# Down projection of a feed-forward layer: seven 2x2-block products in place of eight, for the first four k-tiles of seven column pairs

## The chip, the cores and the metric

The kernel runs on one core of a Trainium2 chip. The metric is the device time of one execution in microseconds (us). TensorE (PE) multiplies matrices into eight PSUM banks of 128 x 512 fp32, VectorE (DVE) and ScalarE (ACT) do elementwise work, GpSimd (POOL) and SyncE (SP) here mostly start transfers, and 16 DMA engines carry these out.

## The reference

Two blocks run one after the other on 256 tokens of width 2048, in fp32. The part that matters is the feed-forward layer at the end of the second block:

```python
        hn = rmsnorm(x, norm_ffn_pre[l])
        u = jnp.square(jax.nn.relu(jnp.einsum('bsd,df->bsf', hn, w_up[l])))
        y = jnp.einsum('bsf,fd->bsd', u, w_down[l])
        x = x + rmsnorm(y, norm_ffn_post[l])
```

Here w_up is 2048 x 8192 and w_down 8192 x 2048. Everything ahead of it (the gated MLP, two attention branches, an mLSTM and their projections) is untouched.

## The kernel before

**Precision.** An fp32 weight is used as two fp32r parts. ACT writes the high part (`wh`, line 561), DVE subtracts it from the weight and writes the low part (`wl`, line 1052). Tokens are kept as high and low parts too (`yth`, `ytl` for the inputs of the down projection). A product takes three matmuls: token high x weight low (line 1931), high x high (1932), token low x weight high (1933).

**Groups.** Weights come in groups of two k-tiles (256 rows) by 512 columns, 512 KB each, by one transfer of SP into one of five `stage` buffers (line 374). With two k-tiles, two halves of the tokens (128 each) and three matmuls, a group is 12 matmuls of 128 x 128 by 512 columns. Group j uses split buffer j modulo 5: ACT's part of group j waits until PE has finished group j-5 (semaphore `used`), DVE's part waits for ACT (`hi`), PE for DVE (`lo`), and the load of group j+5 waits for DVE's part of group j. 914 groups run in a fixed order, a chunk of 512 columns after the other, eight groups to a chunk of 16 k-tiles.

**The feed-forward layer** runs in four blocks q of 2048 hidden columns: chunks ("up", q, 0 to 3), then ("down", q, 0 to 3), which sum over this block's 16 k-tiles. Chunks alternate between PSUM banks 0, 1 and 2, 3, one bank for each half of the tokens. After an up chunk, ACT applies relu and square (lines 1002, 1005), DVE transposes it in 32 x 32 blocks (line 1092), SP sends it with four transfers of 128 KB into `ytl` (line 388), ACT makes the high part `yth` (line 589) and DVE the low one (line 1080). After a down chunk DVE copies or adds the two banks into `dacc` (lines 1801 and 1803); in block 3 it also multiplies by a row of gains (line 1806) that POOL has loaded into `rowb` (line 518).

**Order.** Each engine's program is written out by hand and runs strictly in order. `slot(n)` puts the splits of all groups up to n+3 ahead of the step that follows it, and `end(...)` is the group after a chunk's last. A step that waits holds up all that stands behind it on its engine.

## Time and profile before

| what | value |
|---|---|
| device time, median of 3 runs (lowest to highest) | 2576.77 us (2576.63 to 2576.93) |
| the profiled execution: its time, its span | 2578.93 us, 2577.2 us |
| busy: PE, weight loads of PE, DVE, ACT, POOL | 2571.3, 2131.7, 1582.6, 1246.6, 34.8 us |
| granted TensorE clock | full in all 40 slices |

The span runs from the first to the last instruction that the profiler saw; 1.73 us of the profiled execution lie around it. Busy time of PE is the time in which some matmul is under way, and matmuls overlap, so that the spacing of their starts, not their duration, tells how long one takes. Times in the rows are counted from the start of the span.

### The profile page before, as it was taken

The page shows a single profiled execution, that of the slowest core. Times are in us where ns is not written, and L with a number is a line of the kernel's source. Part 1 is how long each engine was busy: PE and PEld are TensorE (multiplying, and loading weights), DVE is VectorE, ACT ScalarE, POOL GpSimd, SP SyncE. Part 2 cuts the span into 40 slices and gives each one's busy share as a digit, 9 for nine tenths or more (in the row PEclk, how much of TensorE's full clock was granted, in tenths as well). Part 3 has the DMA queues.
Part 4 walks back from the last instruction along what each step waited for, and adds up shares of the span by engine and source line. Part 5 has one row for each costly group of instructions (what it writes and reads, how often), then busy time and mean ns, then how long its engine had stood idle before and what let it go on. Part 6 is the DMA issues. An engine that isn't in the chain of part 4 may idle for free.

```text
span 2577.2 us, 29181 instructions
## 1 busy us (share of the span) xinstructions
PE 2571.3 (100%) x11503; PEld 2131.7 (83%) x11503; DVE 1582.6 (61%) x1842; ACT 1246.6 (48%) x1495; POOL 34.8 (1%) x56
## 2 busy tenths in 40 slices
PE   9999999999999999999999999999999999999999
PEld 7888888888888888888888888888888888888887
DVE  5646565566666566676866876556575555555555
ACT  6554443444555555455544444444464354454453
POOL 1000000000000000000000000000010000000000
PEclk9999999999999999999999999999999999999999
DMA  8767766676777777777565877666566676676674
GB/s 273 205 193 208 205 205 192 199 205 199 216 217 198 211 207 199 223 224 218 168 187 167 222 215 216 203 200 197 192 212 215 194 202 218 186 217 208 196 223 151
DMA packets 534793, 527.41 MB, mean 205 GB/s; under 512 B 294896, under 2 KB 297824, under 8 KB 534656
## 3 DMA queue, kind: packets, MB, share of 16 engines
q1 hardware_dynamic: 531856, 518.09, 67.5%
q0 software_dynamic: 2384, 6.93, 1.1%
q8 instruction: 91, 1.49, 0.2%
q10 hardware_dynamic: 416, 0.52, 0.1%
q14 instruction: 46, 0.38, 0.0%
HBM read 488.24 MB, written 2.10 MB: 190 GB/s over the span
## 4 chain that ended last, share of the span: by engine, by line
PE 99%; DMA 0%; DVE 0%; ACT 0%; issue 0%; SPq 0%
PE bank L1931 32%; PE bank L1933 32%; PE bank L1932 32%; PE bank L2080 1%; PE bank L2069 1%; PE bank L2059 1%; PE bank L2002 0%; DMA t_stage<-in_a_w_in_dram 0%; PE bank L2015 0%; PE bank L2008 0%; PE bank L2140 0%; PE bank L2127 0%; PE bank L1993 0%; PE bank L2160 0%; PE bank L2153 0%; PE bank L2208 0%
## 5 line engine op out<-in xcount | busy, mean ns | idle before, releaser
L1052 DVE TENSOR_TENSOR t_wl<-t_stage,t_wh 128x1024 fp32r<-128x1024 f32 x912 | 1105.5, 1221 | 818.7 <-ACT t_wh L561 816.7
L561 ACT ACTIVATE t_wh<-t_stage 128x1024 fp32r<-128x1024 f32 x913 | 957.2, 1057 | 969.3 <-PE bank L1933 962.4
L1931 PE MATMUL bank<-t_wl,t_xth 128*128 128x512 f32 x2480 | 972.1, 392 | 0.4 <-DVE t_xtl L1073 0.4
L1933 PE MATMUL bank<-t_wh,t_xtl 128*128 128x512 f32 x2480 | 965.2, 389 | 0.0
L1932 PE MATMUL bank<-t_wh,t_xth 128*128 128x512 f32 x2480 | 965.0, 389 | 0.0
L1931 PEld LDWEIGHTS bank<-t_wl,t_xth 128*128 128x128 f32 x2480 | 465.7, 188 | 96.7 <-DVE t_xtl L1073 0.9
L1933 PEld LDWEIGHTS bank<-t_wh,t_xtl 128*128 128x128 f32 x2480 | 465.5, 188 | 96.9
L1932 PEld LDWEIGHTS bank<-t_wh,t_xth 128*128 128x128 f32 x2480 | 465.7, 188 | 96.0 <-issue 0.2
L1931 PE MATMUL bank<-t_wl,t_yth 128*128 128x512 f32 x1026 | 399.2, 389 | 0.0
L1932 PE MATMUL bank<-t_wh,t_yth 128*128 128x512 f32 x1026 | 398.7, 389 | 0.0
L1933 PE MATMUL bank<-t_wh,t_ytl 128*128 128x512 f32 x1026 | 398.7, 389 | 0.0
L1932 PEld LDWEIGHTS bank<-t_wh,t_yth 128*128 128x128 f32 x1026 | 192.6, 188 | 39.9
L1933 PEld LDWEIGHTS bank<-t_wh,t_ytl 128*128 128x128 f32 x1026 | 192.6, 188 | 39.9
L1931 PEld LDWEIGHTS bank<-t_wl,t_yth 128*128 128x128 f32 x1026 | 192.6, 188 | 39.7
L1092 DVE STREAM_TRANSPOSE t_pool<-t_pool 128x512 f32<-128x512 f32 x96 | 99.3, 1073 | 0.0
L1080 DVE SCALAR_TENSOR_TENSOR t_ytl<-t_ytl,t_yth 128x1024 fp32r<-128x1024 f32 x32 | 39.2, 1224 | 57.3 <-ACT t_yth L589 57.1
L589 ACT ACTIVATE t_yth<-t_ytl 128x1024 fp32r<-128x1024 f32 x32 | 33.9, 1061 | 64.2 <-DMA t_ytl<-t_pool 63.8
L1931 PE MATMUL bank<-t_wl,t_mth 128*128 128x512 f32 x128 | 49.9, 390 | 0.0
L1933 PE MATMUL bank<-t_wh,t_mtl 128*128 128x512 f32 x128 | 49.8, 389 | 0.0
L1932 PE MATMUL bank<-t_wh,t_mth 128*128 128x512 f32 x128 | 49.8, 389 | 0.0
L706 ACT ACTIVATE t_pool<-bank,t_scl 128x512 f32<-128x512 f32 x32 | 20.3, 686 | 26.0 <-PE bank L1933 25.9
L1002 ACT ACTIVATE t_pool<-bank,t_scl 128x512 f32<-128x512 f32 x32 | 20.3, 685 | 22.5 <-PE bank L1933 22.4
(304 smaller groups left out, 946.0 us busy)
## 6 DMA issues: line engine op xcount, KB each, us to landing
t_stage<-in_a_w_in_dram SPq DMA_DIRECT2D x192, 512.0 KB, 4.2
t_stage<-in_w_in_dram SPq DMA_DIRECT2D x178, 512.0 KB, 4.3
t_stage<-in_b_w_in_dram SPq DMA_DIRECT2D x128, 512.0 KB, 4.5
t_stage<-in_w_up_dram SPq DMA_DIRECT2D x128, 512.0 KB, 3.9
t_stage<-in_w_down_dram SPq DMA_DIRECT2D x128, 512.0 KB, 4.3
t_stage<-in_a_w_out_dram SPq DMA_DIRECT2D x64, 512.0 KB, 4.1
t_ytl<-t_pool SPq DMA_DIRECT2D x128, 128.0 KB, 3.1
t_stage<-in_b_w_out_dram SPq DMA_DIRECT2D x32, 512.0 KB, 4.5
```

The lines of the kernel that those rows point to most:

```text
L561: e.activation(wh[:, j % N_SPLIT], stage[:, j % N_STAGE], ACT.Copy).then_inc(*hi(j))
L589: e.activation(xh[:, 4 * c:4 * c + 4, :], xl[:, 4 * c:4 * c + 4, :].bitcast(F32), ACT.Copy, scale=scale).then_inc(*xhi(*name))
L706: e.activation(t[:, i, :], accs(name, c)[i], ACT.Copy, scale=scale[:, i:i + 1]).then_inc(*act(name, c, i))
L1052: e.tensor_tensor(low, src, high.bitcast(F32), ALU.subtract).then_inc(*lo(j))
L1080: e.scalar_tensor_tensor(out=low, in0=low.bitcast(F32), scalar=scale, in1=high.bitcast(F32), op0=ALU.mult, op1=ALU.subtract).then_inc(*xlo ...
L1092: e.transpose(turn_out(dst, i), turn_in(src(i))).then_inc(*turned(*name) if i else turned())
L1931: e.matmul(o, h, w_l, start=start, stop=False)
L1932: e.matmul(o, h, w_h, start=False, stop=False)
L1933: return e.matmul(o, l, w_h, start=False, stop=stop)
L2059: last = e.matmul(t[:, part], wst[:, 2 * c + j, :], v_tile(c, i)[:, part], start=True, stop=True)
L2069: last = e.matmul(t[:, nk * j:nk * j + nk], q[:, h, 128 * i:128 * i + 128], k[:, h, 0:nk], start=True, stop=True)
L2080: last = e.matmul(t[:, 128 * j:128 * j + 128], at_[:, from_:from_ + 128], v[:, b, 128 * h:128 * h + 128], start=b == 0, stop=b == i)
```

## The change

For 14 of the 16 down chunks, taken as seven pairs of 512-column neighbours (all but chunks 2 and 3 of block 3), the first four k-tiles are computed in another way. The 256 tokens by 512 rows are cut into a 2 x 2 matrix of blocks A11 to A22 (token half, even or odd k-tiles), the weights of the two chunks into B11 to B22 (even or odd k-tiles, chunk). Their product takes eight block products of two k-tiles, one token half and 512 columns each; the changed kernel forms it with seven, P1 to P7, by Winograd's scheme, out of sums and differences of blocks:

- **Tokens.** Once per block q, DVE forms four sums of blocks (`sums`) from the first up chunk's tokens, ACT and DVE split them into high and low parts.
- **Weights.** P1, P2 and P3 use the loaded blocks B11, B21 and B22. P5, P6, P7 and P4 use differences that DVE forms in place in the stage buffers (`operand`), each from blocks and from the difference before it: B12 - B11, B22 - (that), B22 - B12, B21 - (the second). Each of the seven is split like a group. A product is then 6 matmuls.
- **Order.** P1, P5, P6 and P7 go into banks 4 to 7, between the last four groups of the chunk or pair ahead. P2, P3 and P4 go straight into the banks of the pair, between its first groups. The two chunks of a pair are now interleaved, with k-tiles 4 to 15 left to each.
- **Results.** ACT copies P1 (`apart`, into the buffer `added`) and P5 (into `rowb`), DVE adds the four into the quarters that belong to the four banks (`together`). In block 0 the quarters are written to `dacc` itself. In blocks 1 to 3 POOL adds them into `dacc` by two accumulating transfers of 512 KB per pair, five pairs in all (semaphores `summed`). `down_evac`, which adds the banks to `dacc`, waits for them, and so does the next pair's copy of P1 into `added`.
- **Buffers.** The weight stage gets two more buffers (`ubuf`, free by then), and a load takes the buffer that comes free first, in an order worked out ahead. A pair's four blocks come in four transfers of 512 KB, as the four groups did.

```diff
+def halved_pairs():
+    return [(("down", q, c), ("down", q, c + 1)) for q in range(4) for c in (0, 2) if (q, c) != (3, 2)]
...
+    def groups_of(m):
+        a, b = pairs[m]
+        own = []
+        for n, k in enumerate((4, 6, 8, 10)):
+            own += [(a, k)] + {0: [(m, P2)], 1: [(m, P4)]}.get(n, [])
+            own += [(b, k)] + ([(m, P3)] if n == 0 else [])
+        return own + [(a, 12), (a, 14), (b, 12), (b, 14)]
...
+    for u, (_, own) in enumerate(units):
+        m = units[u + 1][0] if u + 1 < len(units) else None
+        for n, group in enumerate(own):
+            ahead = n - len(own) + 4
+            if m is not None and ahead >= 0:
+                home.append((m, ahead))
+            home.append(group)
...
+    for j, (name, k) in enumerate(home):
+        if (name, k) == (("up", 0, 0), 0):
+            for i in range(N_MORE):
+                idle.append((j - N_STAGE, N_STAGE + i, ("soft_weigh", 1, 2)))
+        if name in place:
+            source[j] = load_of(chunks[place[name]], plain_rows(k, 1024 // chunks[place[name]][5]), j, ("lo", j))
+            continue
+        a, b = (chunks[place[x]] for x in pairs[name])
+        at_ = [where[name, p] for p in range(7)]
+        if k == P1:
+            b11 = load_of(a, spread_rows(0), at_[P4], ("lo", at_[P4]))
+            b12 = load_of(b, spread_rows(0), at_[P7], ("lo", at_[P7]))
+        elif k == P5:
+            b22 = load_of(b, spread_rows(1), at_[P3], ("lo", at_[P3]))
+        elif k == P7:
+            b21 = load_of(a, spread_rows(1), at_[P2] + 0.5, ("t4", name))
+            for p in range(7):
+                source[at_[p]] = {P7: b12, P2: b21, P3: b22}.get(p, b11)
...
+    def quarters(m):
+        _, q, c = pairs[m][0]
+        if q:
+            return [added[:, n] for n in range(4)]
+        return [dacc[:, i, cols(c + n)] for n in range(2) for i in range(2)]
...
+        for m, names in enumerate(pairs):
+            if names[0][1]:
+                e.wait_ge(*vec.at("w", "pair", m))
+                for n, (_, q, c) in enumerate(names):
+                    e.wait_ge(*vec.at("d", q - 1, c, 1))
+                    e.dma_start(dacc[:, :, cols(c)], added[:, 2 * n:2 * n + 2, :],
+                                accum_op=ALU.add).then_inc(*summed[n](m))
...
-                e.wait_ge(*loaded[j % N_STAGE].at(j))
+                n, s = source[j]
+                m, f = home[j]
+                if m not in place and f in (P5, P6, P7, P4):
+                    e.wait_ge(*vec.at({P5: "t1", P6: "t2", P7: "t3", P4: "t4"}[f], m))
+                else:
+                    e.wait_ge(*loaded[s].at(n))
                 if j >= N_SPLIT:
                     e.wait_ge(*used.at(j - N_SPLIT))
-                e.activation(wh[:, j % N_SPLIT], stage[:, j % N_STAGE], ACT.Copy).then_inc(*hi(j))
...
+        def apart(m):
+            slot(where[m, P1] + 1)
+            e.wait_ge(*used.at(where[m, P1]))
+            if m and pairs[m - 1][0][1]:
+                for n in range(2):
+                    e.wait_ge(*summed[n].at(m - 1))
+            e.activation(quarters(m)[0], banks[4], ACT.Copy).then_inc(*act("first", m))
+            slot(where[m, P5] + 1)
+            e.wait_ge(*used.at(where[m, P5]))
+            if m:
+                e.wait_ge(*vec.at("w", "pair", m - 1))
+            else:
+                e.wait_ge(*vec.at("mixed", 2))
+            e.activation(fifth, banks[5], ACT.Copy).then_inc(*act("fifth", m))
...
+        def operand(m, f):
+            t1, t3, t22, t21 = (stage[source[where[m, p]][1]] for p in (P1, P7, P3, P2))
+            if f == P1:
+                n, s = source[where[m, P7]]
+                e.wait_ge(*loaded[s].at(n))
+                e.wait_ge(*lo.at(where[m, P1]))
+                e.tensor_tensor(t1, t3, t1, ALU.subtract).then_inc(*vec("t1", m))
+            elif f == P5:
+                n, s = source[where[m, P3]]
+                e.wait_ge(*loaded[s].at(n))
+                e.wait_ge(*lo.at(where[m, P5]))
+                e.tensor_tensor(t1, t22, t1, ALU.subtract).then_inc(*vec("t2", m))
+            elif f == P6:
+                e.tensor_tensor(t3, t22, t3, ALU.subtract).then_inc(*vec("t3", m))
+            elif f == P2:
+                e.wait_ge(*lo.at(where[m, P6]))
+                e.tensor_tensor(t1, t21, t1, ALU.subtract).then_inc(*vec("t4", m))
...
+        def sums(q):
+            e.wait_ge(*arrived("up", q, 0))
+            t = ytl[:, 0:4, :].bitcast(F32).rearrange("p (n e) (i s) -> p e i n s", e=2, i=2)
+            a11, a21, a12, a22 = t[:, 0, 0], t[:, 0, 1], t[:, 1, 0], t[:, 1, 1]
+            s1, s2, s3, s4 = (sum_raw[:, f].rearrange("p (n s) -> p n s", n=2) for f in range(4))
+            e.tensor_tensor(s1, a21, a22, ALU.add).then_inc(*vec())
+            e.tensor_tensor(s3, a11, a21, ALU.subtract).then_inc(*vec())
+            after_own()
+            e.tensor_tensor(s2, s1, a11, ALU.subtract).then_inc(*vec())
+            after_own()
+            e.tensor_tensor(s4, a12, s2, ALU.subtract).then_inc(*vec("sums", q))
+            after_own()
...
+        def together(m):
+            _, q, c = pairs[m][0]
+            one, three_, two, four_ = quarters(m)
+            slot(where[m, P6] + 1)
+            e.wait_ge(*used.at(where[m, P6]))
+            e.wait_ge(*act.at("first", m))
+            e.tensor_tensor(two, banks[6], one, ALU.add).then_inc(*vec("u2", m))
+            slot(where[m, P7] + 1)
+            e.wait_ge(*used.at(where[m, P7]))
+            e.wait_ge(*vec.at("u2", m))
+            e.tensor_tensor(three_, banks[7], two, ALU.add).then_inc(*vec("u3", m))
+            e.wait_ge(*act.at("fifth", m))
+            e.tensor_tensor(two, two, fifth, ALU.add).then_inc(*vec("v", "pair", m))
+            e.wait_ge(*vec.at("u3", m))
+            e.tensor_tensor(four_, three_, fifth, ALU.add).then_inc(*vec("w", "pair", m))
+        def down_evac(q, c):
+            slot(end("down", q, c))
+            e.wait_ge(*used.at(end("down", q, c) - 1))
+            if q == 3:
+                e.wait_ge(*row_in[c % 2].at("ffn", c))
+            if q and (q, c) != (3, 2):
+                e.wait_ge(*summed[c % 2].at(pair_of["down", q, c]))
+            for i in range(2):
+                d, p = dacc[:, i, cols(c)], accs("down", q, c)[i]
+                e.tensor_tensor(d, d, p, ALU.add).then_inc(*vec("d", q, c, i))
+                if q == 3:
+                    e.wait_ge(*vec.at("d", 3, c, i))
+                    e.tensor_tensor(buf[c][:, i, :], d, rowb[:, c % 2, :], ALU.mult).then_inc(*vec("dr", c, i))
         for q in range(4):
-            for c in range(4):
-                if c:
-                    up_turn(q, c - 1)
...
+        def halved(m, f, j):
+            a, b = pairs[m]
+            bank = {P1: banks[4], P5: banks[5], P6: banks[6], P7: banks[7], P2: accs(*a)[0], P3: accs(*b)[0],
+                    P4: accs(*a)[1]}[f]
+            if f <= P7:
+                bank_of(4 + f)
+                free[4 + f] = (act.at("first", m), act.at("fifth", m), vec.at("u2", m), vec.at("u3", m))[f]
+            if f in (P1, P2):
+                e.wait_ge(*arrival(("down", a[1], 0), 0))
+            elif f == P5:
+                e.wait_ge(*xlo.at("sums", a[1]))
+            for n in range(2):
+                h, l = {P1: (tokens(yth, 2 * n, 0), tokens(ytl, 2 * n, 0)),
+                        P2: (tokens(yth, 2 * n + 1, 0), tokens(ytl, 2 * n + 1, 0)),
+                        P4: (tokens(yth, 2 * n + 1, 1), tokens(ytl, 2 * n + 1, 1)),
+                        P5: (tokens(sum_h, 0, n), tokens(sum_l, 0, n)),
+                        P6: (tokens(sum_h, 1, n), tokens(sum_l, 1, n)),
+                        P7: (tokens(sum_h, 2, n), tokens(sum_l, 2, n)),
+                        P3: (tokens(sum_h, 3, n), tokens(sum_l, 3, n))}[f]
+                w_h, w_l = wh[:, j % N_SPLIT, n, :], wl[:, j % N_SPLIT, n, :]
+                e.matmul(bank, h, w_l, start=n == 0 and f <= P7, stop=False)
+                e.matmul(bank, h, w_h, start=False, stop=False)
+                last = e.matmul(bank, l, w_h, start=False, stop=n == 1 and f <= P7)
+            return last
```

What moves, by engine. On PE, one product that goes between two groups of an up chunk: before, the last rows of a group and the start of the next (tiles `t_xth`, `t_xtl` are the tokens of the up projection, `bank0`, `bank1` a chunk's banks):

```order
L1931 MATMUL bank0<-t_wl_57,t_xth_50 128x512
L1932 MATMUL bank0<-t_wh_56,t_xth_50 128x512
L1933 MATMUL bank0<-t_wh_56,t_xtl_51 128x512
L1931 MATMUL bank1<-t_wl_57,t_xth_50 128x512
L1932 MATMUL bank1<-t_wh_56,t_xth_50 128x512
L1933 MATMUL bank1<-t_wh_56,t_xtl_51 128x512
L1931 MATMUL bank0<-t_wl_57,t_xth_50 128x512 [waits lo]
```

And on PE in the changed kernel, at the last four groups of ("up", 0, 3):

```order
L2126 MATMUL bank1<-t_wh_56,t_xth_50 128x512
L2127 MATMUL bank1<-t_wh_56,t_xtl_51 128x512
L2188 MATMUL bank4<-t_wl_57,t_yth_52 128x512 [waits xlo,lo]
L2189 MATMUL bank4<-t_wh_56,t_yth_52 128x512
L2190 MATMUL bank4<-t_wh_56,t_ytl_53 128x512
L2188 MATMUL bank4<-t_wl_57,t_yth_52 128x512
L2189 MATMUL bank4<-t_wh_56,t_yth_52 128x512
L2190 MATMUL bank4<-t_wh_56,t_ytl_53 128x512
L2125 MATMUL bank0<-t_wl_57,t_xth_50 128x512 [waits lo]
```

P1 stands between two groups with its own wait for the split weights. In all, PE has 42 instructions fewer, DVE 97 more, ACT 39 more, POOL 10 more, and SP as many as before.

On DVE, around the transposes of the last up chunk of a block (`t_pool4`), before (line 1092 is the transpose, line 1080 the low part of the tokens):

```order
L1080 SCALAR_TENSOR_TENSOR t_ytl_53<-t_ytl_53,t_yth_52 128x1024 [waits xhi]
L1052 TENSOR_TENSOR t_wl_57<-t_stage_55,t_wh_56 128x1024 [waits hi] x5
L1092 STREAM_TRANSPOSE t_pool4_58<-t_pool4_58 128x16x32 [waits act]
L1092 STREAM_TRANSPOSE t_pool4_58<-t_pool4_58 128x16x32
L1052 TENSOR_TENSOR t_wl_57<-t_stage_55,t_wh_56 128x1024 [waits hi] x3
L1080 SCALAR_TENSOR_TENSOR t_ytl_53<-t_ytl_53,t_yth_52 128x1024 [waits xhi]
```

And in the changed kernel, at the same place of block 1 (line 1202 is the difference for P7, line 1205 that for P4, lines 1967 to 1975 are `together`):

```order
L1967 TENSOR_TENSOR t_vreg_70<-bank6,t_vreg_70 128x512 [waits act,used]
L1183 TENSOR_TENSOR t_wl_57<-t_stage_55,t_wh_56 128x1024 [waits hi]
L1205 TENSOR_TENSOR t_stage_55<-t_stage_55 128x1024 [waits lo]
L1183 TENSOR_TENSOR t_wl_57<-t_stage_55,t_wh_56 128x1024 [waits hi]
L1971 TENSOR_TENSOR t_vreg_70<-bank7,t_vreg_70 128x512 [waits vec,used]
L1973 TENSOR_TENSOR t_vreg_70<-t_vreg_70,t_rowb_59 128x512 [waits act]
L1975 TENSOR_TENSOR t_vreg_70<-t_vreg_70,t_rowb_59 128x512 [waits vec]
L1183 TENSOR_TENSOR t_wl_57<-t_stage_55,t_wh_56 128x1024 [waits hi]
L1183 TENSOR_TENSOR t_wl_57<-t_ubuf_64,t_wh_56 128x1024 [waits hi]
L1244 STREAM_TRANSPOSE t_pool4_58<-t_pool4_58 128x16x32 [waits act]
L1244 STREAM_TRANSPOSE t_pool4_58<-t_pool4_58 128x16x32
```

The differences and the sums of the products stand among the splits, ahead of the transposes.

On POOL, at the end of its program, before:

```order
L543 TENSOR_SCALAR t_mixout<-t_mixout,t_scl 128x512 [waits vec]
L545 TENSOR_TENSOR t_hres<-t_hres,t_mixout 128x512 [waits pool]
L543 TENSOR_SCALAR t_mixout<-t_mixout,t_scl 128x512 [waits vec]
L545 TENSOR_TENSOR t_hres<-t_hres,t_mixout 128x512 [waits pool]
L518 DMA t_rowb<-in_norm_ffn_post_dram 128x512 [waits vec] x4
```

And in the changed kernel:

```order
L635 TENSOR_SCALAR t_mixout<-t_mixout,t_scl 128x512 [waits vec]
L637 TENSOR_TENSOR t_hres<-t_hres,t_mixout 128x512 [waits pool]
L635 TENSOR_SCALAR t_mixout<-t_mixout,t_scl 128x512 [waits vec]
L637 TENSOR_TENSOR t_hres<-t_hres,t_mixout 128x512 [waits pool]
L644 DMA t_vreg<-t_vreg 128x2x512 [waits vec] x10
L610 DMA t_rowb<-in_norm_ffn_post_dram 128x512 [waits vec] x4
```

The ten accumulating transfers stand ahead of the four rows of gains, which now wait for the last pair's sums.

## Rows read from the trace of the kernel before

**Rows 1.** The page: span, busy time by engine, granted clock in 40 slices.

```profile
span 2577.2 us, 29181 instructions
PE 2571.3 (100%) x11503; PEld 2131.7 (83%) x11503; DVE 1582.6 (61%) x1842; ACT 1246.6 (48%) x1495; POOL 34.8 (1%) x56
PEclk9999999999999999999999999999999999999999
```

**Rows 2.** Windows: block 1 of the feed-forward layer, busy time by engine, clock, DMA.

```profile
2064.00:2238.00 174.00, 174.00 (x770) 144.06 (x769) 94.50 (x84) 79.57 (x81) 0.00 (x0) 1.00 0.67 206
```

**Rows 3.** Groups, 1876-2560 us: count | busy us, mean ns | idle before.

```profile
L1931 PE MATMUL bank<-t_wl,t_yth 128*128 128x512 f32 x498 | 193.7, 389 | 0.0
L1052 DVE TENSOR_TENSOR t_wl<-t_stage,t_wh 128x1024 fp32r<-128x1024 f32 x253 | 306.4, 1225 | 243.1 <-ACT t_wh L561 242.9
L1803 DVE TENSOR_TENSOR t_vreg<-t_vreg,bank 128x512 f32<-128x512 f32 x22 | 14.4, 684 | 3.8 <-PE bank L1933 3.8
L561 ACT ACTIVATE t_wh<-t_stage 128x1024 fp32r<-128x1024 f32 x252 | 262.2, 1056 | 269.6 <-PE bank L1933 267.0 <-DVE t_scl L1107 2.6
```

**Rows 4.** Timeline of PE, two groups' first matmuls: start, duration.

```profile
2134.34 0.39 PE L1931 MATMUL bank<-t_wl,t_yth 128*128 128x512 f32 x1
...
2137.06 0.39 PE L1931 MATMUL bank<-t_wl,t_yth 128*128 128x512 f32 x1
```

**Rows 5.** Timeline of ACT behind two up chunks: start, duration, [idle before].

```profile
2112.78 1.27 ACT L1002 ACTIVATE t_pool<-bank,t_scl 128x512 f32<-128x512 f32 x2 [1.60 <-PE bank L1933]
...
2124.85 1.06 ACT L589 ACTIVATE t_yth<-t_ytl 128x1024 fp32r<-128x1024 f32 x1 [2.79 <-DMA t_ytl<-t_pool]
...
2136.80 2.00 ACT L561 ACTIVATE t_wh<-t_stage 128x1024 fp32r<-128x1024 f32 x2
...
2146.53 1.06 ACT L589 ACTIVATE t_yth<-t_ytl 128x1024 fp32r<-128x1024 f32 x1 [2.71 <-DMA t_ytl<-t_pool]
```

**Rows 6.** Timeline of DVE in the same stretch.

```profile
2137.88 1.23 DVE L1052 TENSOR_TENSOR t_wl<-t_stage,t_wh 128x1024 fp32r<-128x1024 f32 x1 [3.68 <-ACT t_wh L561]
2139.02 2.07 DVE L1092 STREAM_TRANSPOSE t_pool<-t_pool 128x512 f32<-128x512 f32 x2
...
2147.62 1.23 DVE L1080 SCALAR_TENSOR_TENSOR t_ytl<-t_ytl,t_yth 128x1024 fp32r<-128x1024 f32 x1 [2.54 <-ACT t_yth L589]
2148.76 2.35 DVE L1052 TENSOR_TENSOR t_wl<-t_stage,t_wh 128x1024 fp32r<-128x1024 f32 x2
...
2156.30 1.28 DVE L1803 TENSOR_TENSOR t_vreg<-t_vreg,bank 128x512 f32<-128x512 f32 x2 [0.34 <-PE bank L1933]
```

**Rows 7.** Groups of the whole span, nearest to added operations.

```profile
L1718 DVE TENSOR_TENSOR t_pool<-t_pool 128x1024 f32<-128x1024 f32 x4 | 4.9, 1226 | 0.1
L1612 DVE TENSOR_TENSOR t_pool<-t_pool 128x256 f32<-128x256 f32 x16 | 6.8, 425 | 0.5
L700 ACT ACTIVATE t_vreg<-bank 128x512 f32<-128x512 f32 x4 | 2.4, 598 | 10.0 <-PE bank L2080 10.0
```

**Rows 8.** Timeline of SP's queue: start, time to issue, count.

```profile
2141.12 2.97 SPq L388 DMA_DIRECT2D t_ytl<-t_pool  x4
```

**Rows 9.** Windows; last columns: DMA engines' busy share, GB/s.

```profile
2137.60:2140.20 2.60, 2.60 (x13) 2.17 (x12) 2.32 (x3) 1.36 (x3) 0.00 (x0) 1.00 0.04 13
2140.20:2142.40 2.20, 2.20 (x11) 1.81 (x10) 2.20 (x3) 0.90 (x1) 0.00 (x0) 1.00 0.72 234
2142.40:2146.50 4.10, 4.10 (x20) 3.40 (x19) 2.16 (x2) 1.06 (x1) 0.00 (x0) 1.00 0.91 154
2147.00:2150.00 3.00, 3.00 (x15) 2.46 (x14) 2.38 (x3) 2.49 (x3) 0.00 (x0) 1.00 0.98 332
```

**Rows 10.** DMA, 1876-2560 us: queue (packets, MB, share); issues (KB, landing).

```profile
q0 software_dynamic: 320, 1.05, 0.6%
t_stage<-in_w_down_dram SPq DMA_DIRECT2D x128, 512.0 KB, 4.3
```

**Rows 11.** The page's DMA issues: POOL's largest load.

```profile
t_vreg<-in_a_w_s_dram POOLq DMA_DIRECT2D x1, 1024.0 KB, 10.5
```

More of the change, by code:

```diff
@@ L23 @@
 N_STAGE = 5
+N_MORE = 2
 N_SPLIT = 5
+P1, P5, P6, P7, P2, P3, P4 = range(7)
 class Signal:
@@ L153, in _program @@
     hold, _ = sb("hold", [16, S], offset=s_at + 4096 + 2112)
+    stage = [stage_[:, i] for i in range(N_STAGE)] + [ubuf[:, i] for i in range(N_MORE)]
     ident, _ = sb("ident", [128, 128])
@@ L200, in _program @@
     landed = [signal(f"landed{i}", 16) for i in range(4)]
+    summed = [signal(f"summed{i}", 16) for i in range(2)]
     used = signal("used")
@@ L221, in _program @@
     place = {chunk[0]: n for n, chunk in enumerate(chunks)}
-    first, groups, home = {}, [], []
-    for name, w, r0, nk, c0, width in chunks:
-        first[name] = len(groups)
-        per = 1024 // width
-        for k in range(0, nk, per):
-            home.append((name, k))
-            groups.append((w, r0 + 128 * k, c0, width, per))
-    N = len(groups)
+    pairs = halved_pairs()
+    first_of = {a: m for m, (a, b) in enumerate(pairs)}
+    pair_of = {x: m for m, names in enumerate(pairs) for x in names}
@@ new lines, in groups_of @@
+    def groups_of(m):
[5 more added lines that the diff above has]
+        return own + [(a, 12), (a, 14), (b, 12), (b, 14)]
+    units = []
+    for chunk in chunks:
+        name, nk, per = chunk[0], chunk[3], 1024 // chunk[5]
+        if name in first_of:
+            units.append((first_of[name], groups_of(first_of[name])))
+        elif name not in pair_of:
+            units.append((None, [(name, k) for k in range(0, nk, per)]))
@@ new lines, in _program @@
+    home = []
+    for u, (_, own) in enumerate(units):
[5 more added lines that the diff above has]
+            home.append(group)
+    N = len(home)
+    where = {h: j for j, h in enumerate(home)}
+    first = {chunk[0]: where[chunk[0], 4 if chunk[0] in pair_of else 0] for chunk in chunks}
+    loads_, source = [], {}
@@ new lines, in _program, with load_of, plain_rows, rows @@
+    idle = [(-N_STAGE + i, i, None) for i in range(N_STAGE)]
+    def load_of(chunk, rows, freed_at, freed_by):
+        idle.sort()
+        at_, slot_, after = idle.pop(0)
+        name, w, r0, nk, c0, width = chunk
+        loads_.append((rows(w, r0, c0, width), slot_, after, at_, width))
+        idle.append((freed_at, slot_, freed_by))
+        return len(loads_) - 1, slot_
+    def plain_rows(k, per):
+        def rows(w, r0, c0, width):
+            r = r0 + 128 * k
+            return w[r:r + 128 * per, c0:c0 + width].rearrange("(k p) n -> p k n", p=128)
+        return rows
@@ L368, in loads @@
         def loads(upto):
-            while count["load"] <= min(upto, N - 1):
-                j = count["load"]
-                w, r, c0, width, nk = groups[j]
-                if j >= N_STAGE:
-                    e.wait_ge(*lo.at(j - N_STAGE))
-                e.dma_start(wide(stage, j % N_STAGE, width), w[r:r + 128 * nk, c0:c0 + width].rearrange(
-                    "(k p) n -> p k n", p=128)).then_inc(*loaded[j % N_STAGE](j))
+            while count["load"] <= min(upto, len(loads_) - 1):
+                n = count["load"]
+                rows, s, after, _, width = loads_[n]
+                if after is not None:
+                    e.wait_ge(*{"lo": lo, "t4": vec, "soft_weigh": prod}[after[0]].at(
+                        *(after[1:] if after[0] == "lo" else after)))
+                e.dma_start(wide(stage[s], width), rows).then_inc(*loaded[s](n))
                 count["load"] += 1
         def slot(n):
-            loads(n + 8)
+            loads(sum(load[3] <= n + 3 for load in loads_) - 1)
         def send(src, rows, *name):
@@ L1810, in vector @@
+            if ("down", q, 2) in first_of:
+                together(first_of["down", q, 2])
+            down_evac(q, 1)
+            for c in range(2, 3 if q == 3 else 4):
+                down_evac(q, c)
+        e.wait_ge(*square.at("d", 2, 1))
+        partial_sum(partD, ssq, 3, D, "partD")
         slot(N)
@@ L2247, in tensor @@
         name = ("down", 3, 3)
-        products(909)
-        for j in range(909, 914):
+        products(N - 5)
+        for j in range(N - 5, N):
             e.wait_ge(*lo.at(j))
@@ L2252, in tensor @@
         last.then_inc(*half("down", 0))
[L2253 removed]
+        for j in range(N - 5, N - 1):
             last = half_products(name, j, 1, until=14)
```

105 lines of the change are left out of this document (62 added, 43 removed).

## The prediction

> **What bounds the kernel now.** I read the page first, then the stage that the change touches, then single instructions. The page says that PE is busy for 2571.3 of 2577.2 us and that its clock is granted in full in every slice [rows 1]. An average can hide a stage with another limit, so the next view is the windows: in block 1 of the feed-forward layer PE is busy for all 174.00 us, DVE for 94.50, ACT for 79.57, at full clock, with the DMA engines at 0.67 [rows 2]. The groups say the same from the waiting side: PE's matmuls of this layer had 0.0 us of idle time before them, while DVE's splits waited 242.9 us for ACT and ACT's waited 267.0 us for PE [rows 3]. So ACT and DVE run after PE, held by the five split buffers, and the price of a matmul is the spacing of starts on PE: twelve starts from 2134.34 to 2137.06 are 2.72 us, 0.2267 us each [rows 4].
>
> **What is removed.** A product is 6 matmuls. Eight of them were 48 matmuls of a pair's first four k-tiles, seven are 42; seven pairs lose 42 matmuls, 42 x 0.2267 = 9.5 us. PE never waits here, so all of it lies on the path, as long as nothing makes PE wait. No other matmul is added or moved out of this layer. A half group takes 1.36 us on PE.
>
> **What is added, as load.** Per pair: three more splits (1.06 on ACT, 1.22 on DVE), four differences on DVE (nearest row: two SBUF inputs, 128x1024, 1.226), two copies from PSUM on ACT (0.598), four additions of 128x512 on DVE (0.684) [rows 3, 7]. Per block: four small additions (0.425) and one split each way. For a block with two pairs that is 2 x (3.7 + 4.9 + 2.7) + 2.9 = 25.5 us on DVE and 2 x 4.4 + 1.1 = 9.8 us on ACT; DVE goes from 94.5 of 174 us to 120 of some 171, ACT from 79.6 to 89. As sums neither becomes the bound. They could bound locally, so I walked through the two tight stretches, adding durations in queue order. Back to back, a split or difference costs 1.13 us (two take 2.35, one 1.23) and a short addition 0.6 (two take 1.28) [rows 6].
>
> **Stretch 1: P1, P5, P6, P7 between the last groups of an up chunk.** The differences form a chain: each waits for the split of the one before, each split on ACT for its difference. A link is 1.23 + 1.06 + 1.22 = 3.5 us, and PE takes 4.08 us from one product to the next, so the chain keeps up once it has a start. What costs it a lead is the token chunk ahead. With 0 at the group after ("up", 1, 2), which starts 0.2 us ahead of ACT's relu at 2112.78, ACT waited for that chunk until +12.3 [rows 5]. DVE now forms P5's difference ahead of the transposes, so the chunk comes 1.1 later, at +13.4. ACT then ends the high part at +14.5, DVE the low part at +15.6, the split of P6 at +16.8, P7's difference at +17.9, the split of the full group behind P6 at +19.1. PE wants that group at 4 x 2.72 + 1.36 + 2.72 + 1.36 + 2.72 + 1.36 = +20.4. Margin 1.3 us, four times. I take no cost; without that cover each us of delay costs four.
>
> **Stretch 2: the second pair of a block.** Its two chunks are interleaved, so bank pair 0, 1 or 2, 3 of the pair ahead must be emptied soon: PE starts the new pair's second chunk 12.24 us after the last group of the old pair's first chunk (three groups, three products). In that time DVE has, in its queue, two additions for the old first chunk, four splits and P4's difference, the four additions of the products, and the two additions for the old second chunk: 5 x 1.13 + 8 x 0.6 = 10.5, started some 0.4 late. Margin about 1.3 us, three times (blocks 0 to 2). Again no cost, and three us per us of delay.
>
> **Stretch 3: the eighth group after the last up chunk.** Now 0 is 2134.34. Before, the chunk ("up", 1, 3) was transposed at +4.7 to +6.75, sent from +6.8, waited for by ACT until +12.2; its low part ran from +13.3, and the split after it was done at +15.65 [rows 5, 6, 8]. That split is for the eighth group from 0, which PE wanted at 8 x 2.72 = +21.8: a margin of 6.1 us. P2, P3 and P4 stand among these eight now, so PE wants it at 5 x 2.72 + 3 x 1.36 = +17.7. The margin falls to 2.0 us. Transposes and relu stand where they stood, behind the same split, so the chunk is sent as early as before.
>
> **The accumulating transfers** are what fills that margin. From +19.1 of stretch 1 DVE has five more splits, P4's difference and the four additions ahead of it: 19.1 + 6 x 1.13 + 4 x 0.6 = 28.3, with waits for ACT about 29, and 27.2 of that is 0 here. So POOL issues at about +2, 5 us ahead of the send. Bytes of two transfers: 1.05 MB. The trace has no accumulating transfer. Its nearest row is POOL's plain queue in this layer: 1.05 MB took 0.6% of 16 engines over 684 us, 4.1 us of all of them [rows 10]. From below, the cost to the send is 0, if packets of both queues overlap. From above I double the row, 8.2, since an addition also reads its destination (a plain 1024 KB load of POOL needed 10.5 to land, with its start [rows 11]). The engines have room at +3.5 to +8.1, an estimate of 1.5 us for the first bytes: 0.04 busy, then a load at 0.72 over 2.2 us, 1.6 us of work [rows 9]. The changed order puts one more load there, another 1.6. Free: 4.6 - 3.2 = 1.4 us. What is left over meets the send, which had the engines at 0.91 [rows 9]: 4.1 - 1.4 = 2.7 us late, less the margin of 2.0 is 0.7, for the three first pairs of blocks 1 to 3: 2.1 us. At 0 nothing is lost, at 8.2 it is (8.2 - 3.4) x 3 = 14.4. I take 2.1, from the nearest row.
>
> On the doubling there is a rule in the Trainium skill, "Collectives: The Full Stack", section "The bandwidth ceiling: the fold count and why AG ≠ RS ≠ AR": an add in the DMA engine is slower because it needs two source reads, not because of the arithmetic. By that rule the sum would lose 14.4 us, not 2.1; no run here has shown it yet.
>
> **The other waits.** ACT's copy of P1 for a second pair waits for the first pair's transfers, 25 us after their issue; DVE's additions wait for them 30 us after. Both are beyond 10.5 us twice over, so no cost. Weight loads: a load took 4.3 us to land [rows 10], and by the same walk those of the products and of the groups around them are issued 4 us or more ahead of ACT's split, with four further us before PE wants it. POOL's rows of gains come behind the last transfers, 30 us ahead of their use. Tail and start are as before.
>
> **Sum.** -9.5 + 2.1 = -7.4 us. Against the profiled execution: 2578.93 - 7.4 = 2571.5, with 1.73 of it outside the span. The median of the runs is 2.16 below that execution, so 2576.77 - 7.4 = **2569.4 us**.
>
> **Rivals.** Changes within 0.2%, 5.2 us, are about what a measurement of this kernel can tell from none: faster is below 2571.6, slower above 2581.9.
>
> *DVE falls behind in stretches 1 and 2.* For it: margins of 1.3 us rest on sums without a semaphore's delay, and DVE has hardly a pause there. Against it: from ACT's end (2146.53 + 1.06) to DVE's start at 2147.62 there are 0.03 us [rows 5, 6]. At 2 us late everywhere: 4 x 0.7 + 3 x 0.7 = 4.9, 2569.4 + 4.9 = 2574.3. Chance 0.14, no change.
>
> *The transfers cost half as much again.* At a work of 6.2 us a pair: (6.2 - 3.4) x 3 = 8.4, so 2575.7: the gain is taken back by the wait of ACT for the last up chunk. Chance 0.12, no change.
>
> *The transfers read twice and go ahead of the send.* At 8.2 us a pair, with all that is left in front of the chunk's packets: 2576.77 - 9.5 + 14.4 = 2581.7, and slower by 0.2% from a work of 3.4 + 14.7/3 = 8.3 us on. For it: the chunk's 128 KB transfers are many small packets, at 154 GB/s with the engines at 0.91, against 332 GB/s when weight loads run beside them [rows 9]. Against it: this very rise says that two kinds of packets overlap. Chance of being slower 0.12. On the packets' order the Trainium skill ("DMA: Bandwidth & Descriptors", section "SWDGE vs HWDGE vs iDMA") says that an engine turns between its queues in round-robin; by that rule each of the few large packets would wait for one small packet only, and this rival's order would hold.
>
> *Nothing is late.* 2576.77 - 9.5 = 2567.3; it lies within the forecast's own range, 2566.6 to 2571.6.
>
> **Chances.** Faster 0.62, within 0.2% 0.26, slower 0.12. The range has to reach into the middle cases: from 2566.6 (the full gain, and 0.7 for ends that are not modelled) to 2578.0, which takes in both middle rivals and leaves out the slow end.
>
> **What would show it.** Right: 42 matmuls fewer, 0.0 us of PE idle at P1, P5, P6, P7; the last up chunk's high part at about +14 in blocks 1 to 3 and +12 in block 0; at most 1 us of PE waiting at the eighth group. Stretch 1 wrong: PE waits for DVE's split two places behind P6. Stretch 2 wrong: PE waits for DVE's addition to `dacc`. The transfers wrong: their landing, read from POOL's issues, beyond some 10 us a pair, and ACT's wait for the chunk longer by as much. The prediction fails if PE's waits add up to more than 5 us, or if matmuls are not the 0.2267 us apart that they were.

## The result: slower, 2586.27 us

The changed kernel takes **2586.27 us** (median of 6 runs, 2580.84 to 2588.05) against 2576.77 us for the kernel before (6 runs, 2576.62 to 2577.97). The ratio is 1.0033, 95% interval 1.0023 to 1.0043: slower by 9.5 us, where 7.4 us faster was forecast, and above the upper end of the range, 2578.0. The profiled execution took 2585.01 us.

The page of the changed kernel, beside [rows 1]:

```profile
span 2582.8 us, 29347 instructions
PE 2564.4 (99%) x11461; PEld 2124.9 (82%) x11461; DVE 1663.5 (64%) x1939; ACT 1275.5 (49%) x1534; POOL 47.1 (2%) x66
PEclk9999999999999999999999999999999999999999
```

PE has exactly 42 matmuls fewer (11503 to 11461). It is busy for 6.9 us less, while the span is 5.6 us longer, so PE must now be idle somewhere. The slices are too coarse to show where. The groups of the same layer, 1876 to 2560 us, beside [rows 3], do (count | busy us, mean ns | idle before it, and what ended that):

```profile
L2125 PE MATMUL bank<-t_wl,t_yth 128*128 128x512 f32 x379 | 149.5, 394 | 11.7 <-DVE t_wl L1183 11.7
L1183 DVE TENSOR_TENSOR t_wl<-t_stage,t_wh 128x1024 fp32r<-128x1024 f32 x192 | 232.9, 1224 | 115.4 <-ACT t_wh L666 114.4
```

Where [rows 3] had 0.0 us, the first matmul of a group now waited 11.7 us for DVE's split. DVE is not the bound by its load, since its splits have 115.4 us of idle time ahead of them, waiting for ACT. The view of waits says how often (total, times, longest), and shows ACT at the other end of it, waiting for the 16 token chunks:

```profile
PE bank L2125 <- DVE t_wl L1183: 11.7, 3, 4.6
ACT t_yth L694 <- DMA t_ytl<-t_pool: 78.1, 16, 10.8
```

Three waits, one in each of blocks 1 to 3, and none elsewhere. PE's timeline shows the one of block 1 (start, duration; in brackets the idle time before it):

```profile
2152.74 0.39 PE L2127 MATMUL bank<-t_wh,t_ytl 128*128 128x512 f32 x1
2157.25 0.80 PE L2125 MATMUL bank<-t_wl,t_yth 128*128 128x512 f32 x1 [4.12 <-DVE t_wl L1183]
...
2158.27 0.63 PE L2127 MATMUL bank<-t_wh,t_ytl 128*128 128x512 f32 x1
2158.69 0.63 PE L2125 MATMUL bank<-t_wl,t_yth 128*128 128x512 f32 x1
...
2162.53 0.42 PE L2125 MATMUL bank<-t_wl,t_yth 128*128 128x512 f32 x1
```

Read by starts, as in [rows 4]: 2152.74 to 2157.25 is 4.51, of which 0.23 is the matmul itself, so 4.28 us are lost. This is the eighth group behind the last up chunk, the place of stretch 3. Then comes a second loss, which the view of waits doesn't list: the next starts are 0.43 us apart, not 0.2267. Twelve of them, 2157.25 to 2162.53, take 5.28 us where 2.72 is the price, 2.56 us more. The windows give the reason (busy time and count of PE, PEld, DVE, ACT, POOL; then the granted clock, DMA share, GB/s):

```profile
2160.00:2162.00 2.00, 2.00 (x6) 1.62 (x5) 1.90 (x3) 0.00 (x0) 0.00 (x0) 0.50 0.78 272
2164.00:2166.00 2.00, 2.00 (x11) 1.65 (x10) 1.90 (x2) 0.45 (x1) 0.00 (x0) 1.00 0.71 235
```

The granted clock is at half, the 1.2 GHz level, behind the wait, and full again by 2164. By the same reading block 2 lost 3.09 us waiting and 0.1 to the clock, block 3 lost 4.77 and 1.7. Waits 12.1 and clock 4.4 make 16.5 us; less the 9.5 of the matmuls that is +7.0. On the median before, 2576.77 + 7.0 = 2583.8, 1.2 us short of this execution.

**Where the wait comes from.** The chain of the work that ended last, in order of time (start, duration, what), goes from the last matmul of the up chunk, which the chain has at 2135.22, through all that stretch 3 named:

```profile
2135.49 1.28 ACT t_pool L1132 x2
2136.81 0.94 issue
2137.76 1.05 ACT t_wh L666
2138.83 1.23 DVE t_wl L1183
2140.06 2.01 DVE t_pool L1244 x2
2142.09 0.62 SPq L480
2142.75 4.42 SPq L480
2147.22 3.23 SPq L480
2150.49 3.23 DMA t_ytl<-t_pool
2153.74 1.06 ACT t_yth L694
2154.83 1.23 DVE t_ytl L1232
2156.05 1.15 DVE t_wl L1183
2157.25 0.80 PE bank L2125
```

Compute, transposes and the last landing (3.23) are as long as before. What has grown is SP's issuing of the four sends of 128 KB. Its timeline, to be held against [rows 8], with two weight loads and POOL's two accumulating transfers just ahead:

```profile
2138.73 1.73 SPq L467 DMA_DIRECT2D t_stage<-in_w_down_dram  x2
2142.09 9.08 SPq L480 DMA_DIRECT2D t_ytl<-t_pool  x4
```

```profile
2137.88 2.53 POOL L644 DMA_DIRECT2D t_vreg<-t_vreg  x2 [258.46 <-DVE t_vreg L1975]
```

2.97 us became 9.08; in blocks 2 and 3 it was 7.96 and 9.68. In block 0, where there are no such transfers, it was 3.74. In block 3, two loads of rows of gains (256 KB each) follow POOL's transfers at once and add to what stands ahead of the send.

The issue is not all that is late. The packets of the sends are small: before, 4156 of the 4209 packets between 2142.4 and 2146.5 were under 512 B. In the changed kernel there were hardly any between 2142 and 2148, though the first send was issued in 0.62 us, as ever. They came from 2148 on (4192 under 512 B by 2154), when POOL's transfers were nearly through. The view from 2142 to 2148:

```profile
DMA packets 755, 1.48 MB, mean 247 GB/s; under 512 B 32, under 2 KB 32, under 8 KB 755
```

So the four sends of block 1 took longer from issue to landing too, before in the first line, in the changed kernel in the second:

```profile
DMA to landing us min/median/max: 3.0/3.1/3.2
DMA to landing us min/median/max: 3.2/7.0/9.0
```

The DMA view of 1876 to 2560 us, beside [rows 10] (queue 0 is POOL's):

```profile
q0 software_dynamic: 3040, 6.29, 4.8%
t_vreg<-t_vreg POOLq DMA_DIRECT2D x10, 512.0 KB, 9.4
```

### The profile page after: what moved, and what is told of

It is laid out like the page before. It is cut to its first block, busy times and chain, and to the rows that moved or that the text cites. A ratio compares the mean times of both kernels' runs of the same rounds, so it can differ in the third digit from the quotient of the medians.

```text
span 2582.8 us, 29347 instructions
## 1 busy us (share of the span) xinstructions
PE 2564.4 (99%) x11461; PEld 2124.9 (82%) x11461; DVE 1663.5 (64%) x1939; ACT 1275.5 (49%) x1534; POOL 47.1 (2%) x66
## 4 chain that ended last, share of the span: by engine, by line
PE 97%; SPq 1%; DVE 1%; DMA 1%; ACT 0%; issue 0%
PE bank L2125 30%; PE bank L2127 30%; PE bank L2126 30%; SPq L480 1%; PE bank L2190 1%; PE bank L2189 1%; PE bank L2188 1%; PE bank L2307 1%; PE bank L2296 1%; PE bank L2286 1%; DMA t_ytl<-t_pool 0%; DVE t_wl L1183 0%; DVE t_pool L1244 0%; DMA t_stage<-in_a_w_in_dram 0%; PE bank L2229 0%
## 5 line engine op out<-in xcount | busy, mean ns | idle before, releaser
L1183 DVE TENSOR_TENSOR t_wl<-t_stage,t_wh 128x1024 fp32r<-128x1024 f32 x850 | 1030.6, 1221 | 692.1 <-ACT t_wh L666 689.6
L666 ACT ACTIVATE t_wh<-t_stage 128x1024 fp32r<-128x1024 f32 x851 | 892.0, 1057 | 850.3 <-PE bank L2127 824.6
L2125 PE MATMUL bank<-t_wl,t_yth 128*128 128x512 f32 x914 | 357.6, 391 | 11.7 <-DVE t_wl L1183 11.7
L2126 PE MATMUL bank<-t_wh,t_yth 128*128 128x512 f32 x914 | 356.8, 390 | 0.0
L2127 PE MATMUL bank<-t_wh,t_ytl 128*128 128x512 f32 x914 | 356.7, 390 | 0.0
L2125 PEld LDWEIGHTS bank<-t_wl,t_yth 128*128 128x128 f32 x914 | 172.6, 189 | 48.7 <-DVE t_wl L1183 12.9
L2126 PEld LDWEIGHTS bank<-t_wh,t_yth 128*128 128x128 f32 x914 | 172.6, 189 | 35.8
L2127 PEld LDWEIGHTS bank<-t_wh,t_ytl 128*128 128x128 f32 x914 | 172.6, 189 | 35.6
L1183 DVE TENSOR_TENSOR t_wl<-t_ubuf,t_wh 128x1024 fp32r<-128x1024 f32 x83 | 101.4, 1222 | 40.7 <-ACT t_wh L666 40.1
L666 ACT ACTIVATE t_wh<-t_ubuf 128x1024 fp32r<-128x1024 f32 x83 | 87.6, 1056 | 72.6 <-PE bank L2127 60.3
```

Of the source, the lines that this page charges most:

```text
L666: e.activation(wh[:, j % N_SPLIT], stage[s], ACT.Copy).then_inc(*hi(j))
L1183: e.tensor_tensor(low, src, high.bitcast(F32), ALU.subtract).then_inc(*lo(j))
L2125: e.matmul(o, h, w_l, start=start, stop=False)
L2126: e.matmul(o, h, w_h, start=False, stop=False)
L2127: return e.matmul(o, l, w_h, start=False, stop=stop)
```

## The experiments

Each was timed against the kernel before on the same chip (medians 2576.90 and 2577.02 us in its two groups of runs). "High part" is the time from an up chunk's last group to the start of its high part on ACT, the prediction's +12.2, here as the mean over blocks 1 to 3 for the last up chunk; "send" is the mean time that SP needs to issue the four transfers. These three columns are read from one profiled execution each; with plain copies (2579.30 us), before plus transfers (2589.60) and PE kept at work (2583.80) it was slower than the median.

| kernel | median us | ratio [95%] | PE waits us | send us | high part us |
|---|---|---|---|---|---|
| before | 2576.77 | | 0.0 | 2.99 | 12.1 |
| changed | 2586.27 | 1.0033 [1.0023, 1.0043] | 11.7 | 8.91 | 18.2 |
| without the transfers | 2567.95 | 0.9966 [0.9953, 0.9979] | 0 | 3.92 | 13.2 |
| transfers later | 2568.00 | 0.9968 [0.9955, 0.9980] | 0 | 3.74 | 13.1 |
| plain copies | 2574.77 | 0.9992 [0.9983, 1.0001] | 5.5 | 6.83 | 16.2 |
| one transfer later | 2571.97 | 0.9981 [0.9972, 0.9990] | 3.2 | 6.06 | 15.4 |
| before, plus transfers | 2587.10 | 1.0037 [1.0023, 1.0051] | 7.1 | 7.06 | 16.4 |
| PE kept at work | 2581.67 | 1.0018 [1.0009, 1.0028] | 2.7 | 9.36 | 18.8 |
| DVE adds instead | 2568.15 | 0.9966 [0.9953, 0.9979] | 0 | 3.90 | 13.2 |

**1. Without the transfers.** My theory was that the transfers delay the send. The rival was that the seven products themselves are at fault: DVE and ACT late in the new order. POOL's ten transfers and the waits for them are left out.

```diff
...
-                    e.dma_start(dacc[:, :, cols(c)], added[:, 2 * n:2 * n + 2, :],
-                                accum_op=ALU.add).then_inc(*summed[n](m))
...
-                for n in range(2):
-                    e.wait_ge(*summed[n].at(m - 1))
+                e.wait_ge(*vec.at("w", "pair", m - 1))
...
-                e.wait_ge(*summed[c % 2].at(pair_of["down", q, c]))
```

> The ten accumulating transfers are left out (the sums of the first four k-tiles of five pairs never reach dacc, so that part of the output is missing); all else is the changed kernel. Theory (the transfers hold up SP's four sends of the last up chunk in blocks 1 to 3): chunk's high part back to about 12 us after the chunk's last group, no wait of PE there, no lowered clock, all 42 matmuls gained: 2567 to 2569 us. Rival A (the added work of DVE and ACT makes PE wait): as the changed kernel, 2581 to 2588.

2567.95 us: 9.0 below the kernel before, where the 42 matmuls are worth 9.5. The window of block 1, beside [rows 2]:

```profile
2064.00:2238.00 174.00, 174.00 (x769) 144.14 (x768) 118.58 (x112) 89.19 (x94) 0.00 (x0) 1.00 0.68 209
```

PE is busy throughout at full clock, with DVE at 118.58 and ACT at 89.19 us (the prediction had 120 and 89). So the whole loss hangs on the transfers, and the rival falls.

**2. The same transfers, later.** Is it their work, or their place? POOL waits, for the first pair of blocks 1 to 3, until the last up chunk's low part is there.

```diff
                 e.wait_ge(*vec.at("w", "pair", m))
+                if names[0][2] == 0:
+                    e.wait_ge(*xlo.at("up", names[0][1], 3))
```

> POOL issues the transfers of a block's first pair only after the low part of the block's last up chunk is written, so after the sends have landed. Theory: sends undisturbed, transfers land some 10 us later, still ahead of their first reader (ACT's copy of P1, about 12 us later): 2567 to 2570. Rival A: 2581 to 2588. Rival B (the transfers hurt by their traffic wherever they stand, through weight loads): 2574 or more.

2568.00 us, as fast as without them, and 8.9 us faster than the kernel before. In block 1 the send is back at 3.83 us, and POOL issues behind it:

```profile
2141.70 3.83 SPq L480 DMA_DIRECT2D t_ytl<-t_pool  x4
```

```profile
2150.98 2.53 POOL L646 DMA_DIRECT2D t_vreg<-t_vreg  x2 [271.96 <-DVE t_ytl L1234]
```

The same bytes with the same additions cost nothing there. It is the place. This one wait is the mended change.

**3. Plain copies.** Is it the addition, or any transfer of POOL? The transfers overwrite instead of adding, which changes the output.

```diff
-                    e.dma_start(dacc[:, :, cols(c)], added[:, 2 * n:2 * n + 2, :],
-                                accum_op=ALU.add).then_inc(*summed[n](m))
+                    e.dma_start(dacc[:, :, cols(c)], added[:, 2 * n:2 * n + 2, :]).then_inc(*summed[n](m))
```

> The same ten transfers, same bytes and places, as plain copies without the addition (dacc is overwritten, so the output is not the reference's). If the second read of the destination is the price: the send of the last up chunk late by some 3 us instead of 6, PE waits about 1 us three times, 2570 to 2573. If any transfer of POOL of this size holds up SP's sends: late by 5 to 7 us as in the changed kernel, 2581 to 2588. Rival A: 2581 to 2588, with the sends as before.

2574.77 us, between the two expectations: neither holds as it stands. The DMA view, 1876 to 2560 us:

```profile
q0 software_dynamic: 1760, 6.29, 2.6%
t_vreg<-t_vreg POOLq DMA_DIRECT2D x10, 512.0 KB, 7.3
```

The queue took 2.6% where adding took 4.8%; without the transfers it takes 0.5%, for the rows of gains. Of 684 us, and for five pairs, that is (2.6 - 0.5)% x 684 / 5 = 2.9 us of all engines per pair for copying and (4.8 - 0.5)% x 684 / 5 = 5.9 for adding: twice. The Trainium skill's rule that the prediction weighed ("Collectives: The Full Stack", section "The bandwidth ceiling: the fold count and why AG ≠ RS ≠ AR": two source reads for an add) agrees with that factor. But adding also took nearly twice as many packets (3040 against 1760 in the queue, 320 of them for the rows of gains), so the runs don't tell the second read from the packets as its reason. And a copy alone held the send for 6.83 us on average, 2.9 more than without transfers. So the addition makes 2.1 of the 5.0 us, and any transfer of this size makes the rest.

**4. One of the two transfers later.** If the delay goes by the work that is ahead of the send, half of it should do half.

```diff
                 for n, (_, q, c) in enumerate(names):
+                    if n and names[0][2] == 0:
+                        e.wait_ge(*xlo.at("up", q, 3))
```

> Of a first pair's two transfers, one is issued where the change has it, the other after the low part of the last up chunk. Theory: half the bytes ahead of the send, late by about 3 us, less the margin of 2.0: PE waits about 1 us three times, no lowered clock, 2569 to 2573. Rival A: 2581 to 2588.

2571.97 us, as the theory had it. The waits are short (total, times, longest), and the clock stays at full behind each:

```profile
PE bank L2127 <- DVE t_wl L1185: 3.2, 3, 1.4
```

**5. The kernel before, with the transfers added.** The prediction laid half of the trouble on the margin at the eighth group, 6.1 us before and 2.0 after. With 6.1 the transfers should cost little in the old order. At the old place POOL adds unused parts of `mtl` to one another, two transfers of 512 KB in each of blocks 1 to 3.

```diff
...
+        for q in range(1, 4):
+            e.wait_ge(*act.at("squared", q, 3))
+            for n in range(2):
+                if q > 1:
+                    e.wait_ge(*extra[n].at(q - 1))
+                e.dma_start(target(n), parts_of(8 + 4 * n), accum_op=ALU.add).then_inc(*extra[n](q))
...
```

> The kernel before, with two accumulating transfers of 512 KB by POOL between unused buffers, issued after ACT's square of the last up chunk in blocks 1 to 3 (about 2.5 us after the chunk's last group, as in the changed kernel). Theory: the chunk's high part starts at 17 to 19 us after the chunk's last group instead of 12.2, which uses up the margin of 6.1 us that this order has: PE waits 0 to 1 us three times, 2577 to 2580. Rival A: high part at 12 us, 2576.8.

2587.10 us: 10.1 slower than before, against 0 to 3 expected. The expectation failed, and its chain in block 1 says why:

```profile
2140.09 1.94 SPq L390
2142.07 3.24 SPq L390
2145.35 3.21 DMA t_ytl<-t_pool
2148.58 1.07 ACT t_yth L607
2149.67 1.24 DVE t_ytl L1098
2151.04 0.47 PE bank L1949
```

PE doesn't wait for a split. It waits for the low part of the tokens themselves, at group six behind the chunk (counted from 0, as the prediction counts its eighth), the first that uses these tokens. In the old order that group starts at 6 x 2.72 = +16.3, and [rows 6] have the low part done at 2147.62 + 1.23, which is +14.5. The old margin was therefore 1.8 us, not 6.1: I had looked only at the split behind it, at the eighth group. The change did not narrow it; at 2.0 it is much the same. Again half clock follows (2506 to 2508 us in block 3):

```profile
2506.00:2508.00 2.00, 1.53 (x4) 1.27 (x5) 2.00 (x3) 1.92 (x3) 0.00 (x0) 0.50 0.99 354
```

The send took 6.59 and 6.54 us in blocks 1 and 2, 3.6 longer than before. The work ahead of it was much that of the changed kernel: POOL's queue took 3.3% here, so (3.3 - 0.6)% x 684 / 3 = 6.2 us a pair. But SP had issued one weight load just ahead of the sends (at 2137.43 in block 1), not two.

**6. PE kept at work.** Is the half clock a price of its own? On PE, 16 matmuls that nobody uses stand ahead of the eighth group in blocks 1 to 3, 16 x 0.2267 = 3.6 us each time. The waits are then mostly filled, and nothing is gained but the clock.

```diff
+                if name in pair_of and k0 == 8 and name[1] and name[2] == 1:
+                    for _ in range(16):
+                        e.matmul(bank_of(7), tokens(yth, 0, 0),
+                                 yth[:, 0:2, :].rearrange("p a b -> p (a b)"), start=True, stop=True)
                 if name not in place:
                     e.wait_ge(*lo.at(j))
```

> The changed kernel with 16 matmuls without use (128x128 by 512, 3.6 us at full clock) on PE ahead of the eighth group after the last up chunk in blocks 1 to 3, where it waits. Theory (the price is the wait of 3 to 5 us and the half clock behind it): the filler lies within the wait, the wait left over is 0 to 2 us, the clock stays at 1.0, 2580 to 2583. If the clock is no part of the price: as the changed kernel or up to 2 us more, 2585 to 2588.

2581.67 us: with 48 matmuls more it is 4.6 us faster than the changed kernel, about the 4.4 read above. The granted clock over the whole execution was 1.000 in eight of the ten runs and 0.999 in two; in the six of the changed kernel it was 0.996 to 0.999. PE's idle time left (total, times, longest):

```profile
PE bank L2125 <- DVE t_wl L1183: 2.7, 2, 2.0
```

In one place the expectation of a full clock failed. In block 3 of the profiled execution, one of the two at 0.999, the filler left PE a wait of 2.2 us, and half clock followed it:

```profile
2510.00:2512.00 2.00, 2.00 (x6) 1.58 (x7) 2.00 (x3) 2.00 (x3) 0.00 (x0) 0.54 0.94 343
```

The low clock belongs to the idle time of PE, not to the transfers: the send is as late as ever (9.36 us).

**7. DVE adds instead of the transfers.** Does the prediction's walk through DVE's queue hold with still less room? DVE adds the quarters to `dacc` by four additions of 128x512 for each of the five pairs, and POOL issues no transfers of sums.

```diff
...
+        def summed_in(m):
+            _, q, c = pairs[m][0]
+            after_own()
+            for n in range(2):
+                for i in range(2):
+                    slot(where[m, P4] + 1 + 2 * n + i)
+                    d = dacc[:, i, cols(c + n)]
+                    e.tensor_tensor(d, d, added[:, 2 * n + i, :], ALU.add).then_inc(
+                        *(vec("s", "pair", m) if n == i == 1 else vec()))
...
```

> No transfers: DVE adds the four quarters of a pair into dacc, four additions of 128x512 from SBUF between later splits. Theory: sends undisturbed, DVE has 5 x 4 x 0.68 = 14 us more to do in five pairs behind the tight places: 2567 to 2570. Rival A (DVE is the bound in these stretches): 2583 to 2590.

2568.15 us, and in block 1 PE without a gap:

```profile
2064.00:2238.00 174.00, 174.00 (x769) 144.11 (x769) 122.47 (x120) 90.06 (x94) 0.00 (x0) 1.00 0.68 209
```

DVE carries 122.47 of 174 us and still delays nobody. The transfers saved an engine that had the time.

## Why the prediction was wrong

**What is removed: right.** 42 matmuls, and 9.0 (without transfers) of the 9.5 us come out as time.

**What is added, as load: right.** DVE and ACT have 118.58 and 89.19 us in block 1 where 120 and 89 were worked out.

**Stretches 1 and 2: right.** No run shows a wait of PE there. The third up chunk's high part was due at +13.4 and came at +13.5 to +14.2 in the four blocks. Margins of 1.3 us that rest on sums of durations held, so the rival "DVE falls behind" falls.

**Stretch 3: the margin was right, what it was compared with was not.** By 2.0 us of margin the high part may come at +14.2. It came at +18.5, +17.3 and +18.9: 4.3, 3.1 and 4.7 too late, and PE waited 4.28, 3.09 and 4.77. But the step "before: a margin of 6.1 us" was wrong. It followed one reader of the chunk, the split, and missed a nearer one, PE itself. Experiment 5 puts the old margin at 1.8. The error didn't move the forecast, which used the 2.0.

**The accumulating transfers: this step failed, and it decided the result.** The term of 2.1 us in the sum measured 16.5. Its parts:

- *Their work.* 4.1 us per pair were taken, from POOL's plain queue; adding took 5.9. The time of their issue was right: 2137.88 is 2.6 behind the group that ends the chunk, where about 2 was worked out. The right value of the work lay between the bounds 0 and 8.2, near the rival "half as much again" (6.2).
- *How the work meets the send.* From it I took 1.4 us of free room, so that a work of 4.1 made the send 2.7 late. The runs show less room. In blocks 1 and 2 the send took 3.5 us without transfers, 5.0 longer with 5.9 us of work ahead of it, 3.0 longer with 2.9 (copies), 2.8 longer with 5.9 / 2 = 2.95 (one transfer). Nearly all of POOL's work lands in front of the send, as the rival "go ahead of the send" had it. The price it gave, 14.4 for a work of 8.2, is close to the 16.5 measured, but through different sizes: that is luck. Room as such was no mistake. In the old order, where the same working gives 4.6 - 1.6 = 3.0 us, 6.2 - 3.6 = 2.6 us found it (experiment 5).
- *What spoke against that rival.* It was a misreading of [rows 9]. The 332 GB/s from 2147 to 2150 are not sends beside weight loads: ACT had begun on the landed chunk at 2146.53 [rows 5], and of the packets in these 3 us hardly any are small. So nothing in the rows showed two kinds of packets overlapping, and the rival's chance was held down for no reason:

```profile
DMA packets 515, 1.00 MB, mean 332 GB/s; under 512 B 28, under 2 KB 28, under 8 KB 515
```

- *What else holds the send.* Another 0.9 us of its time (2.99 to 3.92) is there without any transfer of sums: 0.5 in blocks 1 and 2, whose origin was not tried, and 1.7 in block 3, where POOL now loads two rows of gains (256 KB each) just ahead of the send, at 2481.20 in experiment 1. The prediction looked at these rows only where they are used. In experiment 2 they come behind the send, and it takes 3.66 there; in experiment 1:

```profile
2485.97 4.74 SPq L480 DMA_DIRECT2D t_ytl<-t_pool  x4
```

- *The price of a late send.* I counted only the excess of the delay over the margin, 0.7 x 3 = 2.1 us. It was 12.1, for the high part was 18.2 - 12.1 = 6.1 us late (5.0 and 0.9 of them the send's), about 4 more than the margin, three times. And 4.4 more went to the half clock behind the waits, which stood in no term. That this is a price of its own is what experiment 6 bears out.

On the order of the packets the prediction cited the Trainium skill ("DMA: Bandwidth & Descriptors", section "SWDGE vs HWDGE vs iDMA") for engines that turn between their queues in round-robin. The trace agrees with it only in part. From 2320 to 2322, in block 2 of the changed kernel, POOL's queue (0) and SP's (1) moved 128 packets each:

```profile
q0 software_dynamic: 128, 0.26, 69.3%
q1 hardware_dynamic: 128, 0.26, 39.1%
```

But in experiment 5, from 2142 to 2144, SP had issued two sends, and the weight load ahead of them landed at 2142.6 (2137.43 and 5.2 to landing); its queue moved only 34:

```profile
q0 software_dynamic: 197, 0.40, 109.5%
q1 hardware_dynamic: 34, 0.02, 4.3%
```

(The shares add up the time of packets that overlap.) What made the small packets wait there is not shown.

**What would show it.** The signs were well chosen: the high part at +14 in blocks 1 to 3 (it was +18), at most 1 us of waiting at the eighth group (11.7), and failure if PE's waits pass 5 us. The landing of POOL's transfers told it too: the median of one, 9.4 us, is below the 10 that was named, but that was for a pair, and in block 1 the second transfer, issued 0.8 us behind the first, landed 11.8 us after its own issue: 12.6 for the pair. ACT's wait for the chunk was 10.33 us where [rows 5] have 2.71. Both transfers of block 1:

```profile
DMA to landing us min/median/max: 8.8/10.3/11.8
```

**What stays open.** Why SP's issue of a send stands still while POOL's transfers are under way (4.42 and 3.23 us in one step) and why the sends' packets wait are not shown. That the delay follows the work ahead of the send rests on three points in the changed order; experiment 5, in the old order, fits only with the room that it had. The runs of the changed kernel spread from 2580.84 to 2588.05 us, and the granted clock of the whole execution from 0.999 to 0.996: 0.003 of 2583 us is 7.7 us, where the times differ by 7.2. So, within the rounding of the clock (0.001 is 2.6 us), the half clock behind the waits accounts for the spread; what decides how often it falls was not tried.

## What to carry to other kernels

A transfer that takes work off an engine is not free because the DMA engines have room on average (0.67 of block 1 in [rows 2]): look at what is issued in the microseconds behind it, and let it wait until a transfer on the path has gone. Here one wait on POOL turned 9.5 us lost into 8.9 us gained. For the margin of any tile, list all its readers and take the nearest. And where PE would wait for some microseconds, count the half clock behind it as well as the wait.
